# Where the scan's first body finds its inputs: later convolutions, end of dt, log decays and B*C products in a two-layer SSD and attention kernel

## The reference

```python
h = rmsnorm(x, norm_g) * (1 + scale) + shift
q, k, v, z_a, xbc, z_s, dt_f, dt_b, g_a, g_s = split_cols(h @ w_in, IN_SPLITS)
xbc = jax.nn.silu(centred_conv(xbc, conv_w, conv_b))       # 5 taps along the tokens
xs, b_ssm, c_ssm = split_cols(xbc, (SSD_WIDTH, BC_WIDTH, BC_WIDTH))
dtf = jax.nn.softplus(dt_f + dt_bias_f)                    # and dtb
acs = jnp.cumsum(dtc * a, axis=2)                          # log decays, forward and backward
cb = jnp.einsum('bcign,bcjgn->bcgij', cc, bc)              # the B*C products, 8 groups
y_diag = jnp.einsum('bcgij,bcgrij,bcjgrp->bcigrp', cb, decay_in, xdt)
```

## Time and profile before

| | |
|---|---|
| median of 3 runs | 2823.64 us (2823.5 to 2824.4) |
| span of the profiled execution | 2823.8 us |
| TensorE busy | 2765.8 us, 98% |
| VectorE busy | 1962.2 us, 69% |
| ScalarE busy | 1482.7 us, 53% |
| GpSimd busy | 186.6 us, 7% |
| mean granted TensorE clock | 0.994 |
| weights' transfers (`raw` from w_in), issue to landing | 3.8 us, 608 of 512 KB |

### The profile page before, as it was taken

One profiled execution on the slowest core, in us unless ns is written; L12 is line 12 of the kernel. 1 busy time (PEld: TensorE's weight loads), 2 busy tenths in 40 slices (PEclk: granted clock), 3 DMA queues, 4 the chain that ended last, 5 costly groups with the idle time before them and its releaser, 6 DMA issues.

```text
span 2823.8 us, 40297 instructions
## 1 busy us (share of the span) xinstructions
PE 2765.8 (98%) x16160; PEld 2352.6 (83%) x16160; DVE 1962.2 (69%) x2434; ACT 1482.7 (53%) x2210; POOL 186.6 (7%) x243
## 2 busy tenths in 40 slices
PE   7999999999999999999999999999999999999998
PEld 4898898888777898877779888888888888897886
DVE  2488888887887445588875788988966644545554
ACT  3356777676333445534334577677744434545443
POOL 0000121111000000000010011111110000000000
PEclk8999999999999999999999999999999999999999
DMA  9944545556887554587895545554466665454664
GB/s 393 338 167 162 171 160 172 173 171 211 317 304 257 201 165 149 165 305 287 324 308 175 179 151 171 171 179 159 164 228 234 249 202 171 160 172 165 208 216 164
DMA packets 166330, 594.16 MB, mean 210 GB/s; under 512 B 19988, under 2 KB 22292, under 8 KB 165760
## 3 DMA queue, kind: packets, MB, share of 16 engines
q1 hardware_dynamic: 155376, 558.24, 56.5%
q0 software_dynamic: 10704, 33.34, 3.9%
q10 hardware_dynamic: 64, 0.02, 0.0%
HBM read 577.85 MB, written 13.66 MB: 209 GB/s over the span
## 4 chain that ended last, share of the span: by engine, by line
PE 89%; DVE 6%; DMA 2%; ACT 1%; issue 1%; SPq 0%; DVEq 0%; POOLq 0%; POOL 0%; ACTq 0%
PE PM L474 19%; PE PM L486 19%; PE PM L475 19%; PE PM L479 7%; PE PM L490 7%; PE PM L480 7%; PE A L753 5%; DMA Zt<-in_w_mod 2%; DVE w_l L452 2%; DVE X L1538 1%; DVE arena L1494 1%; PE PM L750 1%; PE A L750 1%; PE A L898 1%; PE A L505 1%
## 5 line engine op out<-in xcount | busy, mean ns | idle before, releaser
L452 DVE TENSOR_TENSOR w_l<-raw,w_h 128x1024 fp32r<-128x1024 f32 (+1 forms) x880 | 1052.0, 1210 | 726.3 <-ACT w_h L447 719.3
L447 ACT ACTIVATE w_h<-raw 128x1024 fp32r<-128x1024 f32 (+1 forms) x880 | 902.5, 1046 | 733.7 <-PE PM L486 518.9
L474 PE MATMUL PM<-w_h,hT_h 128*128 128x512 f32 x1408 | 562.6, 400 | 2.1 <-issue 1.6
L475 PE MATMUL PM<-w_h,hT_l 128*128 128x512 f32 x1408 | 549.7, 390 | 0.0
L479 PE MATMUL PM<-hT_h,w_h 128*128 128x256 f32 x1920 | 487.5, 292 | 5.1 <-ACT w_h L447 2.6
L480 PE MATMUL PM<-hT_l,w_h 128*128 128x256 f32 x1920 | 470.9, 283 | 0.0
L474 PE MATMUL PM<-w_h,Z 128*128 128x512 f32 x1024 | 403.4, 394 | 3.9 <-DVE arena L1494 2.8
L475 PE MATMUL PM<-w_h,Z 128*128 128x512 f32 x1024 | 399.2, 390 | 0.0
L479 PEld LDWEIGHTS PM<-hT_h,w_h 128*128 128x128 f32 x1920 | 367.4, 191 | 20.1 <-issue 11.4
L486 PE MATMUL PM<-w_l,hT_h 128*128 128x512 f32 x1408 | 377.4, 390 | 0.5 <-DVE w_l L452 0.5
L480 PEld LDWEIGHTS PM<-hT_l,w_h 128*128 128x128 f32 x1920 | 368.2, 192 | 6.2 <-issue 4.8
(11 more groups left out here) (205 smaller groups left out, 2322.9 us busy)
## 6 DMA issues: line engine op xcount, KB each, us to landing
raw<-in_w_in SPq DMA_DIRECT2D x608, 512.0 KB, 3.8
raw<-in_w_ps SPq DMA_DIRECT2D x128, 512.0 KB, 4.6
Zt<-in_w_mod SPq DMA_DIRECT2D x96, 512.0 KB, 13.4
arena<-in_w_mod SPq DMA_DIRECT2D x80, 512.0 KB, 6.3
raw<-in_w_pa SPq DMA_DIRECT2D x64, 512.0 KB, 4.0
raw<-in_w_out SPq DMA_DIRECT2D x64, 512.0 KB, 5.6
arena<-in_states POOLq DMA_DIRECT2D x16, 512.0 KB, 3.7
out_states_out<-arena POOLq DMA_DIRECT2D x16, 512.0 KB, 2.9
```

What stands on the lines that cost most here:

```text
L447: act.activation(w_h[:, k % RING, :, 0:n], half_raw(k, n), ACT.Copy).then_inc(hi_ready, 1)
L452: dve.tensor_tensor(w_l[:, k % RING, :, 0:n], half_raw(k, n), w_h[:, k % RING, :, 0:n].bitcast(F32), ALU.subtract).then_inc(lo_ready, 1)
L474: pe.matmul(tok_out(s), hi[:, kt, tk], wh, start=kt == 0, stop=False, skip_group_check=True)
L475: pe.matmul(tok_out(s), lo[:, kt, tk], wh, start=False, stop=False, skip_group_check=True)
```

## The change

It puts steps into other places of the dictionaries, in both layers; no computation is added or removed. On TensorE the log decays move from half 3 of chunk 3 to half 7, its last, and each `cb(q)` one half later. On ScalarE the SiLU of chunk 1 and the center of chunk 2 move from 36 to 37, `H_hi` from 38 to the body's half 0 (40), the SiLU of chunk 2 from 39 to the body's half 3, with `decays` from 0 to 2, the SiLU of chunk 3 from 5 to 7 and the odd copies one half later. On VectorE `dt_end` moves from 33 to 38, the last taps of chunk 1 from 35 to 36, chunk 2's taps from 37 and 38 to the body's halves 0 and 2, `H_lo` and `cumulative` from 39 to the body's half 1, chunk 3's last taps from 4 to 6, `decay_dt` from 2 to 5 and the even copies one half later.

```diff
--- before.py
+++ after.py
@@ -865,7 +865,7 @@
                         for w in range(2):
                             mm = fp32(A[NH * w:NH * w + NH, 0, ds * P:(ds + 1) * P], SA[:, 8 + ds, :], (Umat, Lmat)[ds // 2], ds == 0)
                     mm.then_inc(s_("acsT_done"), 1)
-                halves(base + PH_BC + 3, "ch", 1, ub + U_BC + 1, hT_h, hT_l, {3: [log_decays]})
+                halves(base + PH_BC + 3, "ch", 1, ub + U_BC + 1, hT_h, hT_l, {7: [log_decays]})
                 end_phase(pe)
 
 
@@ -965,7 +965,7 @@
                     halves(base + PH_SSD + g * 2, "ch", 0, ub + U_SSD + g, hT_h, hT_l, steps)
                     halves(base + PH_SSD + g * 2 + 1, "tok", 1, ub + U_SSD + g, hT_h, hT_l, steps, first=8)
 
-                ssd_body(0, {4 + q: [lambda q=q: cb(q)] for q in range(NG)})
+                ssd_body(0, {5 + q: [lambda q=q: cb(q)] for q in range(NG)})
                 for g in range(1, NG):
                     ssd_body(g, ssd_steps(g - 1))
                 end_phase(pe)
@@ -1204,8 +1204,7 @@
                     act.activation(SA[:, 12:14, :], SA[:, 12:14, :], F.Exp).then_inc(s_("ew_exp"), 1)
 
                 st = {26: [params], 28: [dt_copy], 30: [lambda: center(0)], 31: [dt_exp], 32: [dt_ln],
-                      33: [lambda: bc_silu(0), lambda: center(1)], 36: [lambda: bc_silu(1), lambda: center(2)],
-                      38: [H_hi], 39: [lambda: bc_silu(2)]}
+                      33: [lambda: bc_silu(0), lambda: center(1)], 37: [lambda: bc_silu(1), lambda: center(2)]}
                 if L == 0:
                     for j in range(4):
                         squares_x(j, 0)
@@ -1324,8 +1323,8 @@
                     halves(base + PH_SSD + g * 2, st)
                     halves(base + PH_SSD + g * 2 + 1, st, first=8)
                     ch.reset()
-                ssd_body(0, {0: [decays], 3: [lambda: center(3)], 5: [lambda: bc_silu(3), lambda: end_phase(act)], 8: [lambda: cb_odd(1)], 10: [lambda: cb_odd(3)],
-                             12: [lambda: cb_odd(5)], 14: [lambda: cb_odd(7)]})
+                ssd_body(0, {0: [H_hi], 2: [decays], 3: [lambda: bc_silu(2), lambda: center(3)], 7: [lambda: bc_silu(3), lambda: end_phase(act)], 9: [lambda: cb_odd(1)], 11: [lambda: cb_odd(3)],
+                             13: [lambda: cb_odd(5)], 15: [lambda: cb_odd(7)]})
                 for g in range(1, NG):
                     ssd_body(g, ssd_steps(g - 1))
                 end_phase(act)
@@ -1656,9 +1655,8 @@
                     dve.wait_ge(s_("ew_exp"), L + 1)
                     ch.link(tt(SA[:, 12:14, :], SA[:, 12:14, :], SA[:, 4:8:2, :], ALU.mult))
 
-                st = {27: [params], 31: [dt_abs, lambda: conv_bc(0, 0)], 32: [dt_u, lambda: conv_bc(0, 1)], 33: [dt_end],
-                      34: [lambda: conv_bc(1, 0)], 35: [lambda: conv_bc(1, 1)], 37: [lambda: conv_bc(2, 0)],
-                      38: [lambda: conv_bc(2, 1)], 39: [H_lo, cumulative]}
+                st = {27: [params], 31: [dt_abs, lambda: conv_bc(0, 0)], 32: [dt_u, lambda: conv_bc(0, 1)],
+                      34: [lambda: conv_bc(1, 0)], 36: [lambda: conv_bc(1, 1)], 38: [dt_end], 41: [H_lo, cumulative]}
                 if L == 0:
                     x_rstd(1)
                     for q in range(4):
@@ -1791,8 +1789,8 @@
                     halves(base + PH_SSD + g * 2, st)
                     halves(base + PH_SSD + g * 2 + 1, st, first=8)
                     ch.reset()
-                ssd_body(0, {2: [decay_dt], 4: [lambda: conv_bc(3, 0), lambda: conv_bc(3, 1)], 5: [lambda: end_phase(dve)], 7: [lambda: cb_even(0)], 9: [lambda: cb_even(2)],
-                             11: [lambda: cb_even(4)], 13: [lambda: cb_even(6)]})
+                ssd_body(0, {0: [lambda: conv_bc(2, 0)], 1: st[41], 5: [decay_dt], 2: [lambda: conv_bc(2, 1)], 4: [lambda: conv_bc(3, 0)], 6: [lambda: conv_bc(3, 1), lambda: end_phase(dve)],
+                             8: [lambda: cb_even(0)], 10: [lambda: cb_even(2)], 12: [lambda: cb_even(4)], 14: [lambda: cb_even(6)]})
                 for g in range(1, NG):
                     ssd_body(g, ssd_steps(g - 1))
                 end_phase(dve)
```

## The result

The changed kernel takes 2842.15 us (median of 4 runs, 2840.39 to 2843.49), the kernel before, run beside it, 2824.02 (4 runs): ratio 1.006, with a 95% interval of 1.0047 to 1.0073. That is 18.1 us slower, between 13 and 21. The forecast was 2839.5 with a range of 2833.5 to 2845.0.

The account below looks back on a forecast made before the run. TensorE's own work was taken as the bound (busy 2765.8 of 2823.8 us). Stalls 2 x 6.8 plus clock 2 x 1.9 less 1.6 gave 15.8 us more, 2839.5 us, range 2833.5 to 2845.0.

Parts of the forecast that it names:

- The mechanism: Before half 40, the scan's first, TensorE waits for bank_free[0], counting chunk 2's late taps: 6.8 us more per layer.
- likeliest case: Whole kernel: stall before half 40 plus clock loss in both layers, 15.8 us slower, 2839.5 us; chance 74%.
- Steps 1 to 3: Chunk 3: convolution 0.3 us earlier, waits of 0.75 (half 38) and 1.9 (half 39); loses 2.65 us instead of 3.5.
- Step 4: Before half 40: TensorE idles 8.8 us for the log-decay chain and chunk 2's last taps, starting at 187.3 instead of 180.55.
- Step 5: Behind the stall: the clock falls, 1.9 us lost in each layer, less 1.6 layer 0 already pays: +2.2.
- Rival (c): Behind the stall before half 40: the clock stays up in both layers, 12.0 us slower, 2835.8 us; chance 12%.
- Step 6: Scan body: chunk 3's convolution, later SiLUs, copies, loads and states cost nothing; without cover, at most 2.88 us each.
- rival (d): Scan bodies: VectorE still catching up, one more wait of about 2.9 us in each, 2845.4 us; chance 8%.
- (a): At half 40: the bank wait does not hold, all five waits go, layer 0 keeps its clock, 2814.8 us; chance 3%.
- (b): At half 40: the bank wait does not hold, but chunk 3's 0.75 and 1.9 us waits stay, 2820.1 us; chance 3%.

Follow-up runs that it names:

- the late taps: The kernel before with only the convolutions late as in the changed kernel, end of dt and log decays staying: 2833.56 us, ratio 1.0029.
- the filler's run: The changed kernel with 34 matmuls of 128x512 put into TensorE's wait before half 40 in each layer: 2839.65 us.
- the taps before the chain: The changed kernel with all of chunk 2's taps on VectorE behind low half 39, ahead of H's low part: 2830.07 us, ratio 1.0015.
- the end of dt back: The changed kernel with the end of dt back at 33 and all else late: 2839.54 us.
- one-count experiment: The changed kernel with TensorE's wait at the first scan body asking one count less of bank_free[0]: 2825.36 us, ratio 1.0000.

## Why the prediction was right, step by step

The sum was 15.8 us; the spans differ by 16.9 and the medians by 18.1. The mechanism was right; one term, the clock, was too small. In the likeliest case's own terms:

- The mechanism, the count of `bank_free[0]`, is shown: taken away, the loss goes (2825.36 against 2825.84); alone with the late taps, the stall is there (6.7 us).
- Steps 1 to 3. The wait before half 38 was put at 0.75 and is 0.51; that of half 39 at 1.9, and is 1.79. The 1.27 us wait of half 37 is gone, as said.
- Step 4. TensorE's idle stretch was put at 8.8 and is 8.65 in both layers. From chunk 3's start to half 40 the forecast was 187.3 - 150.65 = 36.65 us; layer 1 has 1587.52 - 1551.09 = 36.4, layer 0 has 188.38 - 150.41 = 38.0. Against 29.9 before, that is 6.5 in layer 1 (forecast 6.8) and 8.1 in layer 0, where the clock is in it.
- Step 5, the clock, is the term that was too small. It was 1.9 twice, less 1.6: 2.2 us. Behind the stall half 40 took 4.80 and 4.94 us instead of 2.88, so 1.9 and 2.1, nearly as taken. What was missed: in layer 0 the clock fell already behind the 1.79 us wait of half 39, so that its low part and the log decays took some 1.5 us more. With that, 1.5 + 1.9 + 2.1 - 1.6 = 3.9 us. With 2 x 6.54 for the stall the sum is 17.0, as the two stretches have it. In the filler's run the same fall hit layer 1 instead, so it is no property of a layer. That 1.9 came out so close is in part luck: it was taken from another stretch of the kernel, and behind the stalls of the other kernels the first work lost between 1.5 and 2.8 us. Rival (c), the clock staying up, is out: with the stall it fell in both layers of every profile that has one (the changed kernel, the taps before the chain, the late taps, the end of dt back). By the Trainium skill's "TensorE: Matmul & The Clock Gate", section "HAM oscillation — how this bites in real kernels", every burst behind a long wait starts cold; the profiles with 6.66 and 8.65 us agree (the clock is at 0.5 when half 40 starts), while behind 3.30 us it fell within half a microsecond of the restart in layer 0.
- Step 6. Nothing else shows: TensorE has no further wait up to 215 us in the changed kernel, and from half 41 of layer 0 to chunk 3 of layer 1 both kernels take 1357.9 us, so rival (d) is out. No wait for chunk 3's SiLU, the states or a load appears.
- Rivals (a) and (b) would have needed the wait for chunk 2 not to hold. The one-count experiment is that case made real, and it comes out 0.5 us below the kernel before of its set, where (a) says 9.0 and (b) 3.7: freed of the bank, halves 44 and 45 wait 0.79 and 0.45 us for what was put later. These rivals' prices left that out.
- The remaining 1.2 us between the difference of the medians and that of the spans fits the trace before being of an execution some 1.6 us slower than the median of its runs, as worked out above. The forecast took that span and the median for the same level. The kernel before alone ran from 2823.01 to 2827.64 in the later runs.

## What to carry to other kernels

Before a step is put later in one engine's order, list every semaphore that it raises and find the first wait for each, counts shared with other buffers included: here chunk 2's taps raised the counter of a bank pair that they never read, and TensorE waited for it. A step that moves must stay ahead of its readers on all engines, and what it moves behind must not itself wait for the reader; then small moves (one or two halves) took out 3 us of waits per layer, where large ones put in 8.65. Count a stall on TensorE at its length plus about 2 us for the first work behind it (1.5 to 2.8 in the four kernels with stalls of 3.3 to 8.65 us).

## What the runs showed that was not expected

- Behind the wait of 1.8 us before low half 39 the clock fell in some places and not in others. Four kernels have this wait in both layers (the changed one, one count less, the filler, the taps before the chain): the clock fell in layer 0 of the changed kernel and in layer 1 with the filler, and stayed up in the other six places, although the work up to there is the same. The run without the wait had no such fall. It cost about 1.5 us each time, so executions of one kernel may well differ by that; no kernel was traced twice to show it.
- With one count less the changed order and the order before take the same time (2825.36 and 2825.84), although nearly every leftover stands elsewhere: the waits moved, 3.7 to 3.8 us per layer.
